# Second mixer: products between the chunks of its projections, key selection beside the first one, divisions deferred or folded

## The reference

```python
cq, ckv, kidx, widx, dq, dk, dv = split_cols(rms_norm(h, norms[i, 1]) @ od_w_in[j], OD_WIDTHS)

# c: attention with chosen keys, 8 heads of 64, key and query from latents
cq = rms_norm(cq, q_norm); ckv = rms_norm(ckv, kv_norm)
q = (cq @ w_uq);  q_idx = (cq @ w_qidx)              # 4 index heads of 64
score = einsum(relu(q_idx . k_idx * 64**-0.5), widx * 4**-0.5)   # per query and key
score = where(visible, score, -inf)                   # key < end of the query's 64-token chunk
_, idx = top_k(score, 128)                            # 128 keys for each query
s = (q_lat . ckv[idx]) * 64**-0.5; o_c = softmax(s) @ ckv[idx] @ w_uv

# d: differential attention, 4 heads, each two softmaxes over 64, values of 128
a = softmax(where(visible, (dq . dk) * 64**-0.5, -inf))
o_d = (a[:, :, 0] - lam * a[:, :, 1]) @ dv            # lam from four small vectors
o_d = rms_norm(o_d, head_norm) * (1 - lam_init)

h = h + concatenate([o_c, o_d]) @ od_w_out[j]
```

## Time and profile before

| | |
|---|---|
| median of three timed runs | 2103.39 us (2099.76 to 2105.74) |
| own time of the profiled execution | 2105.17 us |
| its span | 2103.3 us |
| mean granted PE clock | 0.954 of full speed |
| PE busy | 2016.4 us (96%) |
| PEld busy | 1612.0 us |
| DVE busy | 1036.6 us (49%) |
| ACT busy | 634.5 us (30%) |
| POOL busy | 306.6 us (15%) |

### The profile page before, as it was taken

The page is one execution under the profiler, slowest core; times in us unless marked ns, Lnnn a source line. Parts: engine busy times, 40 slices in busy tenths (PEclk is TensorE's granted clock), DMA queues, the critical chain, the costliest instruction groups (busy, mean ns, idle before and its releaser), DMA issues.

```text
span 2103.3 us, 24455 instructions
## 1 busy us (share of the span) xinstructions
PE 2016.4 (96%) x8908; PEld 1612.0 (77%) x8908; DVE 1036.6 (49%) x1638; ACT 634.5 (30%) x938; POOL 306.6 (15%) x280
## 2 busy tenths in 40 slices
PE   7999999888999999999999999998699999999997
PEld 5888888666788888887888888885455888888886
DVE  5444426861554443346544433455974454443345
ACT  4232222222433222223323222224424333232222
POOL 2000001621400000124000001300334400000124
PEclk9999999885999999999999999999858999999998
DMA  4323232220232323322323232331000222223321
GB/s 159 102 91 99 90 110 80 85 67 21 80 100 90 100 89 110 110 80 90 100 80 110 90 110 91 107 100 41 1 1 7 94 100 93 99 87 110 110 81 50
DMA packets 56732, 179.60 MB, mean 85 GB/s; under 512 B 12145, under 2 KB 12145, under 8 KB 56657
## 3 DMA queue, kind: packets, MB, share of 16 engines
q1 hardware_dynamic: 48032, 171.00, 24.7%
q10 hardware_dynamic: 7712, 4.79, 0.9%
q0 software_dynamic: 928, 3.02, 0.5%
HBM read 175.04 MB, written 3.15 MB: 85 GB/s over the span
## 4 chain that ended last, share of the span: by engine, by line
PE 86%; DVE 8%; POOL 2%; issue 2%; ACT 1%; ACTq 0%; DMA 0%; POOLq 0%; DVEq 0%
PE ps L1516 53%; PE ps L1528 24%; PE ps L1818 2%; PE ps L1854 1%; PE ps L1612 1%; DVE w_lo L309 1%; PE ps L1831 1%; DVE sm L879 1%; DVE work L854 1%; DVE m_b L542 1%; POOL sm L1111 1%; POOL sumsq L1038 1%; DVE stat L852 0%; DVE rstd L343 0%; PE ps L1734 0%
## 5 line engine op out<-in xcount | busy, mean ns | idle before, releaser
L1516 PE MATMUL ps<-x_hi,w_hi 128*128 128x512 f32 x1728 | 683.6, 396 | 28.5 <-DVE x_lo L337 13.1
L1516 PE MATMUL ps<-x_lo,w_hi 128*128 128x512 f32 x1728 | 677.8, 392 | 0.0
L1516 PE MATMUL ps<-x_hi,w_lo 128*128 128x512 f32 x1728 | 677.5, 392 | 0.0
L309 DVE TENSOR_TENSOR w_lo<-raw,w_hi 128x1024 fp32r<-128x1024 f32 x322 | 410.1, 1288 | 473.8 <-ACT w_hi L301 468.1
L301 ACT ACTIVATE w_hi<-raw 128x1024 fp32r<-128x1024 f32 x322 | 332.5, 1050 | 378.1 <-PE ps L1528 314.5
L1516 PEld LDWEIGHTS ps<-x_hi,w_hi 128*128 128x128 f32 x1728 | 327.7, 190 | 104.3 <-issue 18.0
L1516 PEld LDWEIGHTS ps<-x_lo,w_hi 128*128 128x128 f32 x1728 | 328.0, 190 | 69.6 <-issue 2.2
L1516 PEld LDWEIGHTS ps<-x_hi,w_lo 128*128 128x128 f32 x1728 | 327.6, 190 | 68.9
L1528 PE MATMUL ps<-act_hi,w_hi 128*128 (+1 forms) x816 | 319.3, 391 | 2.8 <-DVE act_lo L710 1.4
L1528 PE MATMUL ps<-act_lo,w_hi 128*128 (+1 forms) x816 | 318.4, 390 | 0.0
L1528 PE MATMUL ps<-act_hi,w_lo 128*128 (+1 forms) x816 | 318.4, 390 | 0.0
(11 more groups left out here) (341 smaller groups left out, 1384.3 us busy)
## 6 DMA issues: line engine op xcount, KB each, us to landing
raw<-in_weights SPq DMA_DIRECT2D x322, 512.0 KB, 3.3
h<-in_xT ACTq DMA_DIRECT2D x4, 512.0 KB, 6.9
out<-result SPq DMA_DIRECT2D x4, 512.0 KB, 3.0
p_raw<-in_pT POOLq DMA_DIRECT2D x2, 512.0 KB, 4.0
scratch_u<-u_sc ACTq DMA_DIRECT2D x1, 512.0 KB, 2.8
u_grp<-scratch_u ACTq DMA_DIRECT2D x1, 512.0 KB, 4.2
scratch_y<-y_grp ACTq DMA_DIRECT2D x2, 256.0 KB, 3.3
y_ch<-scratch_y ACTq DMA_DIRECT2D x1, 512.0 KB, 3.5
```

Source lines behind the costliest of these rows:

```text
L309: dve.tensor_tensor(w_lo[:, slot], raw[:, slot], w_hi[:, slot].bitcast(F32), SUB)\
L1516: last = pe.matmul(ps[:, bank], w[:, slot, k], x[:, k], start=(k == 0 and part == 0), stop=(k == KD - 1 and part == 2))
```

## The change

The input chunks keep their first four places (`cq`, `cq`, `ckv`, index), and after them `dq`, `dk`, `dv` come by turns, one head after another (`OD_IN_ORDER`). In this way the first d head is ready after chunk 6. d units now run with the head as the outer loop and the block as the inner one. c units take two heads each, so that there are 16 of them, and 32 units in all. A *group* k holds scores(k), turn(k-2) and values(k-3); groups 0 to 11 stand between the input chunks 7 to 15 (`slot_of_group`, one or two per chunk), and groups 12 to 34 follow the last input chunk. The index queries and index products stand at chunks 4 to 6, the selection rounds (`SELECTS` and one with each group's mask) run beside chunks 5 to 15, and the queries, keys and values of c are made in groups 12 to 17.

The output projection is split: eight tiles over the d channels (`d_tile`, 12 matmuls each), five of them in groups 29 to 33 and three after the last group, whose result is added to the residual on DVE, and then eight tiles over the c channels. The order of its chunks follows (`OD_OUT_ORDER`).

The divisions change: c rows are no longer multiplied by the reciprocal of their sum; `c_scale` divides the product with the values instead, once per block of queries. For d the ratio of the two row sums stands in one factor, and the remaining common factor of a row is left out, since the norm that follows divides by the row's root mean square. POOL's L1111 is gone. The mask step takes a minimum of negated and scaled scores, which is the bias itself, so L883 is gone too. The gains of the latents are multiplied into the small weights once, on POOL. The c value product has the turned probabilities (128 columns) as its weights and the 64 value columns moving; its result has queries on the partitions, and a transpose (`c_turn`) puts it back.

```diff
+OD_IN_ORDER = (0, 1, 2, 3) + tuple(4 * kind + i for i in range(4) for kind in (1, 2, 3))
+OD_OUT_ORDER = ((0, 2), (0, 3), (1, 2), (1, 3), (0, 0), (0, 1), (1, 0), (1, 1))
+D_UNITS = 4 * NQ
+UNITS = D_UNITS + NQ * HEADS // 2
+GROUPS = UNITS + 3
+Z_GROUPS = 12
+C_PREP = tuple([(kind, i) for i in range(4) for kind in ("q", "k")] + [("v", i) for i in range(4)])
...
+D_TURNS = {24: (0, 1), 26: (2, 3)}
+C_TURNS = {29: 0, 31: 1, 33: 2}
+D_TILES = {29: 0, 30: 1, 31: 2, 32: 3, 33: 4}
+LAST_TILES = (5, 6, 7)
+SELECTS = {5: 2, 6: 3, 7: 3, 8: 4, 9: 4, 10: 4, 11: 4, 12: 4, 13: 3, 14: 4, 15: 4}
...
+def slot_of_group(k):
+
+    return 7 + 3 * k // 4
...
+def unit_of(u):
+
+    return ("d",) + divmod(u, NQ) if u < D_UNITS else ("c",) + divmod(u - D_UNITS, HEADS // 2)
...
+            def latents():
+                dve.wait_ge(od_s["std"], 2)
+                for x in (std, sumsq):
+                    dve.reciprocal(x[:], x[:]).then_inc(od_s["rstd"], 1)
+                dve.wait_ge(od_s["rstd"], 2)
+                dve.wait_ge(od_s["qidx_done"], 2)
+                for i, x in enumerate((cq[:, 0], cq[:, 1], ckv[:])):
+                    dve.tensor_tensor(x, x, (std, sumsq)[i // 2][:], MULT)\
+                       .then_inc(od_s["latent"], 1)
...
+                    dve.tensor_tensor_reduce(
+                        out=sm[s % len(sm)][:, 0:keys], in0=ps[:, 2 + s % 2, 0:keys], in1=added,
+                        scale=-SCALE, scalar=-LOWEST, op0=ADD, op1=ALU.min,
+                        accum_out=job[:, 0, s:s + 1]).then_inc(od_s["masked"], 1)
...
+            def c_scale(m):
+                dve.wait_ge(od_s["pv"], D_UNITS + 4 * m + 4)
+                if m >= 2:
+                    dve.wait_ge(od_s["c_turned"], m - 1)
+                jobs = slice(2 * D_UNITS + HEADS * m, 2 * D_UNITS + HEADS * (m + 1))
+                dve.reciprocal(job[:, 3, jobs], job[:, 2, jobs]).then_inc(od_s["c_recip"], 1)
+                dve.wait_ge(od_s["c_recip"], m + 1)
+                dve.tensor_tensor(o_c[:, m % 2].rearrange("p (h d) -> p h d", h=HEADS),
+                                  ps[:, (4, 7)[m % 2]].rearrange("p (h d) -> p h d", h=HEADS),
+                                  job[:, 3, jobs].unsqueeze(2).to_broadcast([P, HEADS, HD]), MULT)\
+                   .then_inc(od_s["c_scaled"], 1)
...
+            for j in range(OD_IN):
+                scale(j)
+                split_lo(dve, first, AHEAD + 2 + j)
+                if j == 4:
+                    lam_sums()
+                if j == 7:
+                    lam_value()
+                if j in (5, 6, 7):
+                    dve.wait_ge(od_s["const"], 2)
+                    combine(j - 5)
+                for k in groups_of_slot(j):
+                    mask(k)
+                    select(1)
+                    mix(k - 1)
+                if j == 13:
+                    latents()
+                select(SELECTS.get(j, 0))
+            for k in range(Z_GROUPS, GROUPS):
+                if k < UNITS:
+                    mask(k)
...
+                mix(k - 1)
+                select(1)
+                if k == D_UNITS + 4:
+                    d_squares()
...
+            pool.wait_ge(od_s["w_loaded"], 16 * 5)
+            pool.wait_ge(param_loaded, 32)
+            for w, at in ((w_qidx[:, 0], 2), (w_qidx[:, 1], 3), (w_uq[:, 0], 2), (w_uq[:, 1], 3),
+                          (w_uk[:], 4), (w_uv[:], 4)):
+                pool.tensor_scalar(w, w, params[:, at:at + 1], None, MULT)\
+                    .then_inc(od_s["w_gained"], 1)
...
+                    pe.wait_ge(od_s["exp"], 2 * u + 2)
+                    pe.wait_ge(od_s["turned_copied"], turns_before(u))
+                    jobs = [(2 * u + n, 5 + n) for n in range(2)]
+                for s, bank in jobs:
+                    for kb in range(blocks):
+                        last = pe.transpose(ps[:, bank, kb * QB:(kb + 1) * QB],
+                                            sm[s % len(sm)][:, kb * QB:(kb + 1) * QB], ident[:])
+                    last.then_inc(od_s["turned"], 1)
...
+                        last = pe.matmul(ps[:, (4, 7)[a % 2], cols],
+                                         pt_c[:, 2 * (u % 2) + n, kb * QB:(kb + 1) * QB],
+                                         v_h[:, kb, cols],
+                                         start=(kb == 0), stop=(kb == blocks - 1))
+                last.then_inc(od_s["pv"], 1)
...
+            for j in range(OD_IN):
+                if j >= 4:
+                    pe.wait_ge(z_ready, zb + (j - 3 if j < 6 else j - 1))
+                in_chunk(pe, first, j, od_bank(j), n=5 if j == 0 else None)
...
+                if j >= 7 and (j - 7) % 3 == 0:
+                    values_in((j - 7) // 3)
+                for k in groups_of_slot(j):
+                    group(k)
+            for k in range(Z_GROUPS, GROUPS):
+                group(k)
+                if k == Z_GROUPS:
+                    values_in(3)
+                if 2 * (k - Z_GROUPS) < len(C_PREP):
+                    c_prep(2 * (k - Z_GROUPS))
+                    c_prep(2 * (k - Z_GROUPS) + 1)
+                for i in D_TURNS.get(k, ()):
+                    d_turn(i)
+                if k in C_TURNS:
+                    c_turn(C_TURNS[k])
+                if k in D_TILES:
+                    d_tile(D_TILES[k])
+            for t in LAST_TILES:
+                d_tile(t)
+            c_turn(NQ - 1)
+            pe.wait_ge(od_s["c_lo"], NQ)
+            for group_ in range(2):
+                place = STARTS[7] + 4 + 2 * group_
+                pe.wait_ge(split_ready, place + 2)
+                if group_:
+                    pe.wait_ge(od_s["part_added"], KD)
+                for d in range(GROUP):
+                    out_tile(place, 0, d, (4, 0)[group_] + d, tile_done)
 
```

More of the change, by code:

```diff
@@ L195, in encoder @@
[L195 to L202 removed]
+        cq = over("cq", [P, 2, T], free_hi)
@@ L940, in od_dve @@
[L940 to L946 removed]
+                if k - 2 in D_TURNS:
+                    for i in D_TURNS[k - 2]:
+                        d_low(i)
@@ L948, in _ @@
+            split_lo(dve, first, OD_IN + 6)
+            split_lo(dve, first, OD_IN + 7)
+            for k in range(KD):
+                update(k)
+                if k:
+                    gained_lo(dve, 6, k - 1)
+                if k == GROUP:
+                    split_lo(dve, first, OD_IN + 8)
+                if k == GROUP + 1:
+                    split_lo(dve, first, OD_IN + 9)
+            gained_lo(dve, 6, KD - 1)
         @block.vector
@@ L1385, in od_act @@
         def od_act(act):
             first = STARTS[6]
-            for j in range(OD_IN):
-                if j != 1:
-                    split_hi(act, first, AHEAD + j)
-                if j == 0:
-                    split_hi(act, first, AHEAD + 1)
-                    root(act, 5)
-                if j == 7:
-                    act.wait_ge(od_s["ssq"], 2)
-                    for i, width in enumerate((2 * P, P)):
-                        act.activation(sm[3 + i][:], ps[:, 5 + i], ACT.Sqrt, bias=eps[:, 0:1],
-                                       scale=1.0 / width).then_inc(od_s["std"], 1)
@@ L1449, in od_act @@
-            block_out(act, "c", NQ - 1)
+                if not 0 <= u < UNITS:
+                    return
+                keys = keys_of(u)
+                if u < D_UNITS:
+                    act.wait_ge(od_s["turned"], u + 1)
+                    if u >= 2:
+                        act.wait_ge(od_s["pv"], u - 1)
+                    act.activation(pt[:, u % 2, 0:keys], ps[:, 5 + u % 2, 0:keys], ACT.Copy)\
+                       .then_inc(od_s["turned_copied"], 1)
+                    return
@@ L1451, in _ @@
+            split_hi(act, first, OD_IN + 4)
+            split_hi(act, first, OD_IN + 5)
+            c_high(NQ - 1)
+            split_hi(act, first, OD_IN + 6)
+            split_hi(act, first, OD_IN + 7)
+            for k in range(KD):
+                gained_hi(act, 6, k)
+                if k == GROUP:
+                    split_hi(act, first, OD_IN + 8)
+                    split_hi(act, first, OD_IN + 9)
         @block.scalar
@@ L1883, in od_pe, with d_turn @@
-            values(len(UNITS) - 1)
+                last.then_inc(od_s["c_prep"], 1)
+            def d_turn(i):
+                pe.wait_ge(od_s["d_scaled"], i + 1)
+                if i < 2:
+                    pe.wait_ge(od_s["c_prep_read"], len(C_PREP))
+                else:
+                    pe.wait_ge(od_s["d_lo"], i - 1)
+                for m in range(NQ):
+                    last = pe.transpose(ps[:, i % 2, m * QB:(m + 1) * QB],
+                                        o_d[:, i, m * P:(m + 1) * P], ident[:])
+                last.then_inc(od_s["d_turned"], 1)
@@ new lines, in c_turn, with out_tile @@
+            def c_turn(m):
+                pe.wait_ge(od_s["c_scaled"], m + 1)
+                if m:
+                    pe.wait_ge(od_s["c_lo"], m)
+                else:
```

(19 more changed lines are left out.)

810 lines of the change are left out of this document (447 added, 363 removed).

## The result

The changed kernel takes 2070.78 us in the median (2068.75 to 2072.18), the kernel before 2104.54 us (2099.76 to 2105.74) beside it: a ratio of 0.9843 with a 95% interval of 0.9824 to 0.9862, so some 33 us less. The forecast was 2086 us in a range of 2064 to 2110. The sign is right and the time lies in the range, but the gain is nearly twice the 17.8 us of the sum, and the case that came is the first rival (2074, clock at full in the c groups), which had a chance of 20%.

What follows compares the result with a forecast made beforehand. DVE was taken to bound chunks 7 to 15 and PE the rest; the terms ended the output projection at 1652.3 instead of 1670.1, a gain of 17.8 us, so 2086 us forecast, range 2064 to 2110.

Steps and rivals of the forecast that it cites:

- the first rival: Clock stays at full through the c groups: 2074 us, down to 2064 with cheap 64-column products; chance 20%.
- Until chunk 7: Input projection from 1349 to 1404.7: PE sets the pace, and the index and latent products are only moved.
- Chunks 7 to 15: Rest of input projection: DVE bounds with 117.6 us plus 2 of stalls, PE idles some 50, ending about 1524.3.
- Groups 12 to 34: Behind the input projection: PE's 84.5 us of passes plus 6 of waits less 4.5 make 86, to 1610.3.
- allowance for the clock: In the c groups: 10 us (0 to 25) added for stretches at low clock, to 1620.3.
- the second rival: Clock at half through all of groups 18 to 28: 15 us more, 2101; chance 20%.
- Tail: Three d tiles, last c scaling and turn, eight c tiles: 32.0 us, output projection ending at 1652.3.
- Start: Start of the second mixer's input projection, taken as 1349 from the old profile.
- The division: POOL's division, 1.62 us for a row of 512 in each c unit, goes; its removal priced at nothing.
- Pairs: 20 pairs of scores in groups 12 to 34 at a mean of 0.815 us (1.13 at 512 keys): 16.3 us.

Runs made afterwards that it cites:

- late13: Changed kernel with 13 of the 48 selection rounds, closing steps included, moved from chunks 8 to 15 into groups 12 to 24, one each: 2062.35 us.
- none_beside: Changed kernel with no selection round beside the input projection; one per group from group 12, missing ones at each block's first mask: 2093.76 us.
- wide_moving: Changed kernel with c's value product in the old form, 64 value columns as weights and 128 turned-probability columns moving: 2070.40 us.
- unpaired: Changed kernel with the two score products of a c unit separated by the turn of group k-2: 2085.13 us.
- both: Changed kernel with the edits of unpaired and wide_moving together, both older forms in the c groups: 2080.17 us.
- before_dense: Kernel before the change with eight dense passes, results unused, added after the turn of unit 26: 2102.87 us.
- before_swap: Kernel before the change with the new form of c's value product, turned probabilities as weights and 64 value columns moving: 2103.49 us.
- pool_back: Changed kernel with a GpSimd multiplication by the row sum between exponential and turn of every c job: 2076.00 us.
- stall: Changed kernel with two unused DVE reciprocals of 128x512 ahead of the mask of group 22: 2078.09 us.
- late13_d: As late13, but the 13 late rounds stand two in each of groups 12 to 18, as far as they go: 2064.03 us.
- late7: As late13, but with 7 late rounds, one in each of groups 12 to 18: 2069.95 us.

## Why the prediction was right in sign and too small in size

**Until chunk 7**: 55.7 us from the projection's start in the sum, and 1402.3 - 1346.6 = 55.7 in the trace.

**Chunks 7 to 15**: DVE's sum and stalls came to 119.6 us; in the trace the last slot's selection ends at 1520.17, 117.9 us behind chunk 7. That DVE sets the pace there was tested by late13 and none_beside. Two side claims were wrong. I let the last input chunk end with DVE's work, at 1515 to 1530; PE's last chunk ended at 1498.2, because in each slot it stands ahead of the groups, and PE waited for masks and not for scalings. And I expected a clock around 1.0 there; it was 0.80. PE had 79 busy of 117 us, so that the waits for DVE probably cover it; no run tried it apart. The exponentials took ACT 0.40 to 0.72 us, not 0.3 to 0.6, which changed nothing.

**Groups 12 to 34**: this is the step that failed. The sum was 86 us and 10 us of allowance for the clock; the trace has 1604.38 - 1520.17 = 84.2. The 86 of instructions and waits stand within 2 us; the 10 taken from the earlier trace rows were not spent, since the clock was 1.00 throughout. The stretch of 68 us at 0.50 was carried over to the new c groups in part, as if it came with their instructions; wide_moving, unpaired and both show that it doesn't come with the forms of the products. The table load that the second rival named is there too, 1.28 us each at 1551.11 and 1553.19, and the clock stayed at 1.00.

The Trainium skill's rule ("TensorE: Matmul & The Clock Gate", Part 4: PE-mode transpose), that transposes don't count as busy, made the low clock look likely; by the rival beside it the time would have been 2101. The trace does not bear it out as the cause here: from 1544 to 1574, ahead of any d tile, 64 of 200 matmuls were transposes (L2029 and L2100), a third, and the clock was 1.00, with PE busy 27.3 of 30 us. In the old stretch at 0.50 (1529 to 1597) they were 40 of 187, a fifth and not the third that the prediction read. The rows of these two stretches, changed kernel first:

```profile
L2029 PE MATMUL ps<-ident,sm 128*128 128x128 f32 x48 | 7.8, 285 | 2.3 <-ACT pt_c L1536 2.3
L2100 PE MATMUL ps<-ident,o_d 128*128 128x128 f32 x16 | 2.3, 276 | 0.4 <-DVE act_lo L983 0.3
```

```profile
L1831 PE MATMUL ps<-ident,sm 128*128 128x128 f32 x40 | 13.2, 444 | 3.6 <-POOL sm L1111 3.6
```

**Tail**: 32.0 in the sum, 32.2 in the trace (1604.38 to 1636.60).

**Start**: the mixer starts 2.5 us earlier (1346.64 against 1349.12). The code ahead of it is the same, and in the other traces it starts between 1343.1 and 1347.8, in those of before_dense and before_swap at 1345.9 and 1344.7: scatter of single executions, which the sum counted as nothing, so that these 2.5 us need not be the change's.

These terms add up: -2.5, 0, -1.7, -11.8, +0.2 are -15.8, and 17.8 + 15.8 = 33.6, against 1670.08 - 1636.60 = 33.5.

**The division**: priced at nothing, since "in the c stretch PE didn't wait for it". That was a misreading: the 3.58 us that PE was not busy in the 68 us of the earlier trace rows are the wait for L1111 at 1533.46. Apart from it the waits stand where the clock was full: 0.55 to 0.60 us ahead of 1529, 0.45 and 0.98 behind 1597, none from 1533.5 to 1597 at half clock. pool_back puts the pass at some 5 us in the new order. So the cover that the prediction relied on came in part from the slow clock.

**Pairs**: I took every pair at the price of a d pair, 1.13 us at 512 keys, and so had the overlap in the sum without seeing it as a term. That the sum came out needed it: unpaired shows that it is 14 us.

**Open**: why the c units before stayed at 0.50 through 60 us of unbroken work, while c groups of the changed kernel regain 1.00 by themselves, 6 to 10 us behind a stall in late13 and stall, 15 in late13_d and 20 in late7. So how much of the 33 us is the clock and how much the order stays open too. Left as differences are that a c unit had one head, that GpSimd stood between exponential and turn, and the order of the work; none was tried alone in the kernel before, and whether the kernel both would regain a lost clock wasn't tried either.

## What to carry to other kernels

Before adding an allowance for a low clock, or trusting a cover that was read beside one, ask whether the instructions themselves or the waits around them were seen to cause it; here a stretch at half clock also hid a slower engine, so the price of its passes has to be read at full clock. Work of a second engine placed beside a projection helped until that engine's own sum was the length of the stretch; spreading it further paid (late13), as long as no piece was longer than the next group could wait (late13_d, late7, none_beside). Two products that use half of TensorE's rows each belong back to back.

## What was not expected of the hardware

- Two matmuls of 64 channels on different halves of the rows, back to back, took 0.71 us together for 256 columns where one alone took 0.70; apart they cost 14 us more over 16 pairs (unpaired).
- The clock fell to 0.50 from 1.00 with waits of only 0.32 and 0.46 us before it (before_dense), yet stayed at 1.00 in the kernel called both, whose scores, transposes and value products have the same forms.
- With 64 weight columns and 128 moving, 160 value passes were busy 15.3 us, with 128 and 64 they were busy 19.6. In the changed kernel's order that is worth nothing (2070.40 and 2070.78 us); with the scores apart it may be worth 5 (2080.17 and 2085.13).
- Full clock came back after 6 to 20 us of work at 0.50 in c groups of much the same make (late13, stall, late13_d, late7).
